# Conditioning partly summed on VectorE, and three pieces of work put elsewhere, in a two-block transformer kernel on one core

## The reference, cut to what matters

```python
silu_c, silu_cc = silu(c), silu(c_ctx)
sh1, sc1, g1, sh2, sc2, g2       = split(silu_c  @ ada_w[i] + ada_b[i], 6)
csh1, csc1, cg1, csh2, csc2, cg2 = split(silu_cc @ ada_w[i] + ada_b[i], 6)
h  = rmsnorm(x,  norm_mix[i]) * (1 + sc1)  + sh1
hc = rmsnorm(xc, norm_mix[i]) * (1 + csc1) + csh1
y, yc = attention(h, hc)               # q, k, v projections; q and k are rotated in layer 0
x  = x  + g1 * y
x  = x  + g2 * conv_ffn(rmsnorm(x, norm_ffn[i]) * (1 + sc2) + sh2)    # the context likewise in layer 0
...
# second block, each layer: one wide projection of the norm, cut into q, kv, gates, ...
proj = rmsnorm_2(x, norm_g) @ w_in
logf = log_sigmoid(f_logit + f_bias); c = cumsum(logf)   # decay of the last mixer
s = q @ k + c[query] - c[key]                            # its causal scores
```

## Time and profile before

| what | value |
|---|---|
| median of 3 runs | 1595.04 us (1594.56 to 1595.25) |
| profiled execution | 1595.22 us |
| its span in the trace | 1593.4 us |
| PE busy | 1568.6 us, 98% |
| DVE, ACT, POOL busy | 59%, 47%, 34% |
| mean granted clock of TensorE | 0.997 |

### The profile page before, as it was taken

How to read it: one execution, slowest core, us unless ns; L and a number is a source line. 1 busy time by engine, 2 the same in 40 slices (tenths; PEclk the granted TensorE clock), 3 DMA queues, 4 the chain that set the end, 5 groups by cost and what they waited for, 6 DMA issues and landing times.

```text
span 1593.4 us, 23097 instructions
## 1 busy us (share of the span) xinstructions
PE 1568.6 (98%) x9146; PEld 1303.4 (82%) x9146; DVE 936.4 (59%) x1441; ACT 750.5 (47%) x1360; POOL 543.3 (34%) x354
## 2 busy tenths in 40 slices
PE   8999999999999999999999999999999999999998
PEld 5778557778887888879768899989998889998887
DVE  4434485555575554342266888757876457968435
ACT  5324485444322433243375755445654445654444
POOL 2224243322211222212273111007424657623663
PEclk9999999999999999999999999999999999999999
DMA  9264500534174222364313754454534534633551
GB/s 393 94 246 187 212 30 9 204 135 157 63 268 184 80 81 73 124 207 164 123 37 113 267 192 172 162 190 170 183 133 161 199 143 171 215 133 132 185 211 54
DMA packets 52603, 249.17 MB, mean 156 GB/s; under 512 B 20624, under 2 KB 21008, under 8 KB 26256
## 3 DMA queue, kind: packets, MB, share of 16 engines
q1 hardware_dynamic: 43744, 243.90, 42.2%
q10 hardware_dynamic: 8752, 3.80, 1.0%
HBM read 246.63 MB, written 1.05 MB: 155 GB/s over the span
## 4 chain that ended last, share of the span: by engine, by line
PE 88%; DVE 5%; ACT 3%; issue 1%; DMA 1%; POOL 1%; SPq 0%; POOLq 0%; ACTq 0%; DVEq 0%
PE psq L554 16%; PE psq L555 16%; PE psq L556 16%; PE ps L554 7%; PE ps L556 7%; PE ps L555 7%; PE psq L970 3%; PE ps L568 1%; PE psq L971 1%; PE ps L970 1%; DMA RAW<-wstream 1%; ACT WHL L526 1%; PE psq L1365 1%; PE ps L1393 1%; PE psq L2298 1%
## 5 line engine op out<-in xcount | busy, mean ns | idle before, releaser
L536 DVE TENSOR_TENSOR WHL<-RAW,WHL 128x1024 fp32r<-128x1024 f32 (+3 forms) x264 | 324.9, 1254 | 290.1 <-ACT WHL L526 289.6
L536 POOL TENSOR_TENSOR WHL<-RAW,WHL 128x1024 fp32r<-128x1024 f32 (+2 forms) x116 | 304.5, 2627 | 504.6 <-ACT WHL L526 471.8
L526 ACT ACTIVATE WHL<-RAW 128x1024 fp32r<-128x1024 f32 (+2 forms) x380 | 361.4, 1002 | 196.1 <-DMA RAW<-wstream 98.6
L554 PE MATMUL psq<-NHL,WHL 128*128 128x256 f32 (+1 forms) x1072 | 353.8, 330 | 1.7 <-POOL WHL L536 0.7
L555 PE MATMUL psq<-NHL,WHL 128*128 128x256 f32 (+1 forms) x1072 | 349.0, 326 | 0.0
L556 PE MATMUL psq<-NHL,WHL 128*128 128x256 f32 (+1 forms) x1072 | 348.9, 325 | 0.0
L554 PEld LDWEIGHTS psq<-NHL,WHL 128*128 128x128 f32 x1072 | 205.2, 191 | 28.9 <-issue 7.5
L556 PEld LDWEIGHTS psq<-NHL,WHL 128*128 128x128 f32 x1072 | 205.3, 191 | 16.6
L555 PEld LDWEIGHTS psq<-NHL,WHL 128*128 128x128 f32 x1072 | 205.3, 191 | 15.4
L554 PE MATMUL psq<-WHL,NHL 128*128 128x512 f32 (+1 forms) x320 | 124.8, 390 | 1.7 <-DVE WHL L536 1.7
L556 PE MATMUL psq<-WHL,NHL 128*128 128x512 f32 (+1 forms) x320 | 123.3, 385 | 0.0
(11 more groups left out here) (389 smaller groups left out, 2975.6 us busy)
## 6 DMA issues: line engine op xcount, KB each, us to landing
RAW<-wstream SPq DMA_DIRECT2D x194, 1024.0 KB, 4.8
RAW<-wstream SPq DMA_DIRECT2D x32, 704.0 KB, 4.0
K<-first SPq DMA_DIRECT2D x4, 1024.0 KB, 17.2
RAW<-wstream SPq DMA_DIRECT2D x4, 800.0 KB, 4.3
X<-xin SPq DMA_DIRECT2D x2, 1024.0 KB, 6.1
V<-first SPq DMA_DIRECT2D x2, 1024.0 KB, 19.3
Q<-first SPq DMA_DIRECT2D x2, 1024.0 KB, 24.7
BR<-rpb ACTq DMA_DIRECT2D x8, 256.0 KB, 8.2
```

Of the source, the lines that this page charges most:

```text
L526: e.activation(WH[:, u % 3, a:z], RAW[:, v % 3, a:z], ACT.Copy).then_inc(w_hi, 1)
L536: e.tensor_tensor(WL[:, u % 3, a:z], RAW[:, v % 3, a:z], WH[:, u % 3, a:z].bitcast(F32), ALU.subtract).then_inc(w_lo_p if pool else w_lo_v, 1)
L554: e.matmul(o, lh, rh, start=start, stop=False)
```

## The change

It has three parts.

- **Conditioning.** For b = 1, units 0, 1, 6 and 7 are summed on DVE, once for each of the two vectors, and units 2 to 5 stay on PE, two behind qkv 5 and two behind qkv 6. For b = 3, units 4 to 7 are summed on DVE, beside up units 1, 3, 5 and 7. The joint product has then two sums and 16 records, with a column of ones in `CB`; that of b = 1 stands ahead of the second value unit and that of b = 3 ahead of up unit 8. For b = 5 and b = 6 all four units stay on PE, some of them earlier by a place. The stream's order follows: behind qkv 3 it has a0, qkv 4, a1, qkv 5, a2, a3, qkv 6, a4, a5, qkv 7, 8 and 9, a6, qkv 10, a7, qkv 11, where it had a0, a1, qkv 4, a2, a3, qkv 5, a4, a5, qkv 6, a6, qkv 7, a7, qkv 8 to 11 (a0 is unit 0 of b = 1). `CB` is cleared by POOL and no longer by DVE.
- **Norm and decay keys.** In the second block the value unit's low part is issued within the norm's loop, at tile 3, and ACT copies `KF` behind the next `split_hi`.
- **First causal product.** It stands between the two halves of g2.

The diff, without declarations of semaphores and tiles and the edits that only follow these (`qkv` and `wo` loops of b = 6, the stream's places for b = 6, where `CB` is waited for):

```diff
@@ -135,10 +135,15 @@
-UP_ADA = {("up", 0, 0): (0, 1, 2, 3), ("up", 0, 2): (4,), ("up", 0, 3): (5,), ("up", 0, 4): (6,), ("up", 0, 5): (7,)}
-QKV_ADA = {("qkv", 1, 4): (0, 1, 2), ("qkv", 1, 5): (3,)}
-JOINT_ADA = {("up", 0, HALF_FT + 1): (7,)}
-LATE_ADA = {("up", 1, 0): (0, 1, 2), ("up", 1, 1): (3,)}
+FIRST_ADA = {3: (0,), 4: (1,), 5: (2, 3), 6: (4, 5), 9: (6,), 10: (7,)}
+FIRST_SUMMED = {1: (0,), 2: (1,)}
+FIRST_ON_PE = {5: (2, 3), 6: (4, 5)}
+UP_ADA = {("up", 0, 0): (0, 1, 2, 3)}
+UP_SUMMED = {1: 4, 3: 5, 5: 6, 7: 7}
+QKV_ADA = {("qkv", 1, 4): (0, 1, 2, 3)}
+LATE_ADA = {("up", 1, 0): (0, 1, 2, 3)}
+SUMMED = {1: (0, 1, 6, 7), 3: (4, 5, 6, 7), 4: tuple(range(8))}
+JOINT_AT = {("qkv", 0, 9): 1, ("up", 0, 8): 3, ("up", 0, HALF_FT + 1): 4}
@@ -163,15 +168,12 @@
-    late_ada = iter(range(DT))
-    for i in range(8):
-        add(("qkv", 0, i), 1 if i < 3 else 2)
-        for _ in range((0, 0, 0, 2, 2, 2, 1, 1)[i]):
-            k = next(late_ada)
+    for i in range(12):
+        add(("qkv", 0, i), 1 if i < 3 or i >= 8 else 2)
+        for k in FIRST_ADA.get(i, ()):
             add_ada(1, k)
+        for k in FIRST_ON_PE.get(i, ()):
             run_ada(1, k)
-    for i in range(4):
-        add(("qkv", 0, 8 + i), 1)
@@ -182,7 +184,7 @@
         add(("up", 0, j), 2)
-        for k in {1: range(4), 2: (4,), 3: (5,), 4: (6,), 5: (7,)}.get(j, ()):
+        for k in {1: range(4), 2: (4,), 4: (5,), 6: (6,), 8: (7,)}.get(j, ()):
@@ -225,10 +227,13 @@
             add(("out", l, i), 1)
-    for name, at, b in (("up", UP_ADA, 3), ("qkv", QKV_ADA, 5), ("up", LATE_ADA, 6), ("up", JOINT_ADA, 4)):
+    for at, b in ((UP_ADA, 3), (QKV_ADA, 5), (LATE_ADA, 6)):
...
             runs[r:r] = [("ada", b, k) for k in ks]
+    for key, b in JOINT_AT.items():
+        r = runs.index(key)
+        runs[r:r] = [("joint", b)]
@@ -294,6 +299,13 @@
+ADA_ACC = {}
+acc_count = 0
+for b_, ks_ in SUMMED.items():
+    for k_ in ks_:
+        acc_count += 1 if b_ == 4 else 2
+        ADA_ACC["ada", b_, k_] = acc_count
@@ -501,8 +514,8 @@
             size = SHAPE[v][0] * SHAPE[v][1]
-            if v >= 3 and KEYS[v - 3][:2] == ("ada", 4):
-                e.wait_ge(ada_acc, KEYS[v - 3][2] + 1)
+            if v >= 3 and KEYS[v - 3] in ADA_ACC:
+                e.wait_ge(ada_acc, ADA_ACC[KEYS[v - 3]])
@@ -558,7 +571,7 @@
             v = UNIT_OF["ada", b, k]
-            if k == 0 and b == 1:
+            if b == 1 and k == 2:
@@ -566,29 +579,44 @@
                 mm = e.matmul(AB[32 * j:32 * j + 32, :], CB[:, c, :], RAW[:, v % 3, 512 * j:512 * j + 512],
-                              start=k == 0, stop=k == ada_units(b) - 1)
+                              start=k == (2 if b == 1 else 0), stop=k == ada_units(b) - 1)
...
-        def dve_ada_step(e, k):
-            v = UNIT_OF["ada", 4, k]
+        def weight_sums(b):
+            if b == 1:
+                return [t.rearrange("p a n -> p (a n)") for t in (PP[:, 3:7, :], TMP[:, 4:8, :])]
+            return [WSUM[:, c, :] for c in range(1 if b == 4 else 2)]
...
+        def dve_ada_step(e, b, k):
+            v = UNIT_OF["ada", b, k]
+            sums = weight_sums(b)
+            at = ADA_ACC["ada", b, k] - len(sums)
             e.wait_ge(d_raw[v % 3], 16 * (v // 3 + 1))
-            if k == 0:
-                e.tensor_scalar(WSUM[:, :], RAW[:, v % 3, :], CB[:, k, 0:1], None, ALU.mult).then_inc(ada_acc, 1)
-                return
-            e.wait_ge(ada_acc, k)
-            e.scalar_tensor_tensor(out=WSUM[:, :], in0=RAW[:, v % 3, :], scalar=CB[:, k, 0:1], in1=WSUM[:, :],
-                                   op0=ALU.mult, op1=ALU.add).then_inc(ada_acc, 1)
...
-        def pe_ada_joint(e):
-            e.wait_ge(ada_par, 3)
-            e.wait_ge(ada_acc, 8)
-            for j in range(4):
-                mm = e.matmul(AB[32 * j:32 * j + 32, :], ONE.to_broadcast([P, 32]), WSUM[:, 512 * j:512 * j + 512],
-                              start=True, stop=True)
+            if b == 4 and k == 0:
+                e.wait_ge(gemm, product(("joint", 3)))
+            for c, t in enumerate(sums):
+                if k == SUMMED[b][0]:
+                    e.tensor_scalar(t, RAW[:, v % 3, :], CB[:, k, c:c + 1], None, ALU.mult).then_inc(ada_acc, 1)
+                    continue
+                e.wait_ge(ada_acc, at - len(sums) + c + 1)
+                e.scalar_tensor_tensor(out=t, in0=RAW[:, v % 3, :], scalar=CB[:, k, c:c + 1], in1=t,
+                                       op0=ALU.mult, op1=ALU.add).then_inc(ada_acc, 1)
...
+        CBF = CB[:, :, :].rearrange("p k n -> p (k n)")
+        ONE_AT = (CBF[:, 16:48], CBF[:, 15:47])
...
+        def pe_ada_joint(e, b):
+            if b == 4:
+                e.wait_ge(ada_par, 3)
+            e.wait_ge(ada_acc, ADA_ACC["ada", b, SUMMED[b][-1]])
+            for c, t in enumerate(weight_sums(b)):
+                for j in range(4):
+                    mm = e.matmul(AB[32 * j:32 * j + 32, :], ONE_AT[c], t[:, 512 * j:512 * j + 512], start=b == 4,
+                                  stop=b == 4 or c == 1)
...
         def act_ada_row(e, b):
-            e.wait_ge(gemm, product(("ada", b, ada_units(b) - 1)))
+            e.wait_ge(gemm, product(("joint", b) if b in SUMMED else ("ada", b, ada_units(b) - 1)))
@@ -926,11 +954,12 @@
-        def pe_wide(e, key, outs, T, xh, xl, wait_x):
+        def pe_wide(e, key, outs, T, xh, xl, wait_x, js=(0, 1)):
...
             nk = SHAPE[v][0]
-            for j, o in enumerate(outs):
+            for j in js:
+                o = outs[j]
@@ -1020,10 +1048,12 @@
                 if l == 0:
-                    for _ in range((0, 0, 0, 2, 2, 2, 1, 1)[i]):
-                        pe_ada(e, 1, next(late_ada))
+                    for k in FIRST_ON_PE.get(i, ()):
+                        pe_ada(e, 1, k)
...
                 if l == 0 and i == 1:
+                    pe_ada_joint(e, 1)
+                if l == 0 and i == 2:
@@ -1074,7 +1104,6 @@
                 if l == 0 and i == 7:
-                    act_ada_row(e, 1)
@@ -1090,9 +1119,14 @@
                     split_hi(e, ahead(key))
+                if l == 0 and i == 0:
+                    act_ada_row(e, 1)
...
             for u, i in enumerate(QKV_ORDER[l]):
+                if l == 0:
+                    for k in FIRST_SUMMED.get(i, ()):
+                        dve_ada_step(e, 1, k)
@@ -1107,8 +1141,12 @@
                     e.tensor_tensor(dst[:, m, 0:256], dst[:, m, 0:256], s, ALU.add).then_inc(rot_v, 1)
-            dve_ada(e, 1 if l == 0 else 5)
+            if l == 0:
+                dve_ada_step(e, 1, 6)
+                dve_ada_step(e, 1, 7)
             for i in range(3):
+                if i == (1 if l == 0 else 0):
+                    dve_ada(e, 1 if l == 0 else 5)
@@ -1509,6 +1547,7 @@
                     pe_ada(e, 6, 0)
+                    pe_ada(e, 6, 1)
@@ -1597,17 +1636,19 @@
                     if l == 0 and c == 0:
-                        for k in UP_ADA.get(("up", 0, jj), ()):
-                            if k > 1:
-                                pe_ada(e, 3, k)
+                        if jj == 0:
+                            pe_ada(e, 3, 2)
+                            pe_ada(e, 3, 3)
+                        if jj == 8:
+                            pe_ada_joint(e, 3)
...
                     if l == 0 and c == 1 and jj == 1:
-                        pe_ada_joint(e)
+                        pe_ada_joint(e, 4)
...
                         pe_ada_turn(e, 4)
-                    if l == 1 and j < 2:
-                        pe_ada(e, 6, 2 + j)
+                    if l == 1 and j == 0:
+                        pe_ada(e, 6, 3)
@@ -1705,6 +1746,8 @@
                     U, key = 22 * l + j, ("up", l, j)
+                    if l == 0 and j in UP_SUMMED:
+                        dve_ada_step(e, 3, UP_SUMMED[j])
@@ -1846,10 +1889,11 @@
-        def pe_proj(e, l, name):
-            pe_ring_free(e, l, name)
+        def pe_proj(e, l, name, js=(0, 1)):
+            if 0 in js:
+                pe_ring_free(e, l, name)
             b = ring_bank(name)
-            pe_wide(e, unit_key(l, name), [b[:, 0:256], b[:, 256:512]], 256, NH, NL, nothing)
+            pe_wide(e, unit_key(l, name), [b[:, 0:256], b[:, 256:512]], 256, NH, NL, nothing, js)
@@ -1908,7 +1952,8 @@
                     dve_raw_out(e, l, "kc")
-            lo_prep(e, l, "qn", False)
+                if m == 3:
+                    lo_prep(e, l, "qn", False)
@@ -1997,7 +2042,6 @@
             act_out_of(e, l, "qf", QF[:, :, :], 0.125)
-            act_out_of(e, l, "kf", KF[:, :, :])
@@ -2089,6 +2133,8 @@
                 split_hi(e, ahead(("cmp", l, kind)))
+                if kind == 0:
+                    act_out_of(e, l, "kf", KF[:, :, :])
@@ -2813,8 +2859,9 @@
             pe_compress_sum(e, l)
+            pe_proj(e, l, "g2", (0,))
             pe_causal_qk(e, l, 0)
-            pe_gates(e, l, 2)
+            pe_proj(e, l, "g2", (1,))
@@ -3078,6 +3124,9 @@
         def pool_start(e):
```

(19 more changed lines are left out.)

## The result

| | before | after |
|---|---|---|
| median | 1595.04 us (1594.56 to 1595.25) | 1606.62 us (1605.73 to 1608.02) |
| ratio | | 1.0074, 95% interval 1.0056 to 1.0091 |
| span of the profiled execution | 1593.4 us | 1604.4 us |
| mean granted clock | 0.997 | 0.993 |

The change made the kernel 0.74% slower, 11.6 us. The forecast was 1598.0 in a range up to 1601.5: slower was the side given most (0.45), but the loss is four times what was summed, and outside the range.

A forecast was written before the change was run, and what follows sets the result against it. The prediction took PE, busy for 98% of the span, as the bound. Gains of 9.6 us and losses of 12.5 made net +2.9 on the profiled 1595.22, hence 1598.0 us, with a range of 1591 to 1601.5.

The forecast's parts named there:

- The wait at the joint: First stage, b = 1: PE waits at the joint product for DVE's four sums; 11.1 us read, 10.5 taken as loss.
- The clock behind that wait: First stage: TensorE runs at half clock after idling at the joint product; loss 2.0 us, bounds 1.7 to 3.4.
- b = 1, 3, 5 and 6 on PE: Conditioning units leaving or moving on PE: gains of 2.0, 2.1, 0.5 and 0.1 us.
- Part 2: Second block, value unit's low part earlier and decay keys copied later: gain 1.0 us a layer, 2.0 in all.
- Part 3: Second block, first causal product between the halves of g2: half clock there goes, gain 2.9 us.
- Rival 3: Second block's waits only move: the norm and decay keys gain 0.3, not 2.0; 1599.7 us, chance 0.1.
- Rival 2: Clock falls all the same at the first causal product, half a unit later: +2.9, 1601 us, chance 0.2.
- rivals 2 to 4: Rival 2, Rival 3 and a fourth: dearer wait at the joint, clock down twice as long, 1601.5 us, chance 0.05.
- rival 1: First stage: DVE is done sooner, so the wait at the joint is 6.0 us; 1592.5 us, chance 0.2.

The follow-up runs named there:

- e7: Changed kernel with 42 products of 512 columns that nobody reads put on PE ahead of the first joint product: 1603.35 us, ratio 1.0050.
- e8: Kernel before with only the decay keys' copy moved behind the high part: 1597.65 us, ratio 1.0013.
- e11: e8 with a further clearing of a scratch tile on POOL ahead of its colliding low part: 1595.15 us, ratio 1.0000.
- e6: e5 with the value unit's low part issued within the norm: 1589.92 us, ratio 0.9965 to the kernel before.
- e10: Kernel before with only the first causal product moved between the halves of g2: 1596.45 us, ratio 1.0009.
- e4: Changed kernel with the first causal product ahead of all of g2 again: 1604.80 us, ratio 1.0061 to the kernel before.
- e5: Changed kernel with the first joint product one value unit later and the second block as before the change: 1590.99 us, ratio 0.9972 to the kernel before.
- e2: Kernel before with the norm, decay keys and causal product edits, conditioning as before: 1595.52 us, ratio 1.0004.
- e3: Changed kernel with the decay keys copied ahead of the high part again: 1603.86 us, ratio 1.0055 to the kernel before.
- e12: e6 with DVE's product for the convolution ahead of the weighting of the compressed scores: 1588.40 us, ratio 0.9961 to the kernel before.

## Why the prediction was wrong

- **The wait at the joint** was right in mechanism, place and size. Read off were 11.1 us, taken 10.5, measured 11.8. The step "I stay near the chain as it is, and take 10.5" took 0.6 off without need.
- **The clock behind that wait**: taken 2.0 us, with 1.7 to 3.4 as bounds. Measured 1.7 us on the joint product and 1.0 on value unit 1, 2.7 in all. The Trainium skill (TensorE: Matmul & The Clock Gate, part 1, the HAM clock gate) says that an idle TensorE drops to 1.2 GHz; the trace agrees, and e7 shows that it is the idling. Only the size was low, by 0.7 us.
- **b = 1, 3, 5 and 6 on PE** were about right: b = 3 won 2.8 instead of 2.1 (each unit taken from between the up units saved 1.2 us of the lag, not 0.99), b = 5 1.0 instead of 0.5; b = 6 lost 0.4, since a unit's load was now waited for (0.96 us) and the low part too (0.82).
- **Part 2, the step that failed.** "So this chain gains about 0.5 too" took `KF` out of ACT's row and counted POOL's earlier start as gain. It left out who else uses that moment. Before, POOL's part began at 1118.45 and DVE's at 1118.47, as good as together, and DVE's went at its own speed (1.21 us). With POOL 0.4 us ahead, DVE's part, wanted first by PE, takes 3.39. e8 and e11 show it: the later copy of the keys alone costs 2.2 us by the medians. The other half of this term, the value unit's low part, gained about 1 us (e6).
- **Part 3, the other step that failed.** "If the clock then stays up, the 1.7 us come back in each layer": they did, as 1.3 us a layer in e10's trace, at that place. What is late next was not asked. It is DVE's product for the convolution, with 0.3 us of slack in the last layer and 0.1 in the first. PE coming 1.3 us sooner waits there, behind a run of small products, and the clock falls there instead. So the 2.9 us of the sum became a loss of 1.4 to 1.8 by the medians (e10, e4), neither clear of no change.
- **The rivals.** Rival 3 (the waits only move) describes what happened in the second block, at a higher price than given: it was priced as a gain that fails to come, not as a loss. Rival 2 (the clock falls all the same) had the cost but not the place: the clock did not fall at the causal product but behind the new waits. The range followed from these prices and ended at 1601.5.
- **The chances.** They don't follow from their own text. Half of the forecast's 0.45, rivals 2 to 4 (0.35) and nothing of rival 1 make 0.575 for slower, not 0.45; the same comes to 0.325 and faster to 0.10.

In the traces, the failed terms of the second block make 7.0 us in the changed kernel, and the first stage 1.5. The three edits of the second block don't add: on the kernel before, the keys alone cost 2.2 us and the split alone 1.4, the value unit's part gained 1.1 on top of e5, and the three together cost 0.4 (e8, e10, e6, e2). In the first layer, PE waits 1.18 us at the convolution's product with the split alone, and 0.22 us in e2, where it has already lost 2.2 at g1. A wait that is taken away there uncovers the next one, as e3 shows.

**What stays open.** Which execution has a fall of the clock in the second block is not fixed by the order of the work alone. The kernel before has a half-clock stretch behind both causal products; e6, in which that product is as whole, has none in its profiled execution, and e5 has one at the second product and one at 1190. So a stretch of 1.3 to 1.5 us that one trace shows is not a sure gain or loss, and the runs of one kernel scatter by about as much (1605.7 to 1608.0 after the change). The profiled executions of e2, e3, e5 and e10 are 1.4 to 3.2 us above their medians, so their traces probably show more of these stretches than most of their runs had.

## What to carry to other kernels

A sum that moves off the critical engine is only cheap where its consumer does not stand right behind the producer's last piece of work: read from the producer's timeline when it will be done, and put the consumer after that. One unit's place was worth 14.6 us here. When a wait is taken away, read which engine is next to be late and by how little; a gain larger than that slack ends there, and an idle moment among small products can cost as much again in clock. And where two engines work side by side on the same memory, an edit that shifts one by half a microsecond can swap which of them is slowed: compare their start times, not only their durations.

## What the runs showed of the hardware

- DVE's and POOL's products over tiles of two operands do not share time evenly. With POOL first by 0.42 us, DVE's 1024 columns took 3.38 us and POOL's 2.72; with DVE first by 0.01 us, they took 1.21 and 3.44 (e8, e11). The turn lies between 0.02 us, where POOL's recorded start was ahead and DVE's part still took 1.21 (before), and 0.06 us, where DVE's took 3.4. A small product is held too: 60 columns took 2.04 us beside POOL's low part (before, 1443.03).
- DVE's product with one operand in PSUM was not held: 0.68 us with POOL's low part begun 0.15 us ahead (e12), as without it (before, 1445.25).
- TensorE, idle from 134.70, had its clock at 1.00 in the window from 136 and at 0.56 in that from 138, and ran its first 5 us of work behind the wait at half (the joint product 3.6 us instead of 1.85). 42 products that nobody reads kept it at 1.00 while they ran; behind them PE idled for 2.1 us, and the windows from 146 and 148 show 0.92 and 0.50 (e7).
- The clock also fell without a long idle: a wait of 0.77 us behind 5 us of products of 15 to 256 columns was followed by half clock in the windows from 1456 (0.50) and 1458 (0.70).
- The same kernel can have such falls in one run and none in another: e10's runs have a mean granted clock of 1.000 at 1594.60 and 1594.70 us, and 0.997 at 1597.81 to 1598.68.
